# A gated delta recurrence: the state read through the keys, and its 16x16 inverses carried in another order

## The reference, cut to what matters

```python
    kb = kc * bc[..., None]
    lower = jnp.where(strict, jnp.einsum('nbhid,nbhjd->nbhij', kb, kc) * decay, 0.0)
    eye = jnp.broadcast_to(jnp.eye(CHUNK, dtype=F32), lower.shape)
    rhs = jnp.concatenate([vc * bc[..., None], kb * jnp.exp(gcum)[..., None]], axis=-1)
    sol = lax.linalg.triangular_solve(eye + lower, rhs, left_side=True, lower=True, unit_diagonal=True)
    u, w = sol[..., :dv], sol[..., dv:]
    ...
    def step(S, inp):
        q_i, k_i, u_i, w_i, a_i, g_i = inp
        v_new = u_i - jnp.einsum('bhck,bhkv->bhcv', w_i, S)
        o = (jnp.einsum('bhck,bhkv->bhcv', q_i * jnp.exp(g_i)[..., None], S)
             + jnp.einsum('bhij,bhjv->bhiv', a_i, v_new))
        g_last = g_i[..., -1]
        S = (S * jnp.exp(g_last)[..., None, None]
             + jnp.einsum('bhck,bhcv->bhkv', k_i * jnp.exp(g_last[..., None] - g_i)[..., None], v_new))
        return S, o
```

## Time and profile before

| what | before |
|---|---|
| median of 3 runs | 4209.69 us (4206.33 to 4217.25) |
| the profiled execution | 4213.43 us, its span 4211.7 us |
| PE busy | 3824.5 us (91%) |
| DVE, ACT, GpSimd busy | 43%, 23%, 8% |
| mean granted clock of PE | 0.951 |
| the two recurrences, from the start of pair 0 to the last product | about 210 us each |

### The profile page before, as it was taken

How to read it: one execution, slowest core, us unless ns; L and a number is a source line. 1 busy time by engine, 2 the same in 40 slices (tenths; PEclk the granted TensorE clock), 3 DMA queues, 4 the chain that set the end, 5 groups by cost and what they waited for, 6 DMA issues and landing times.

```text
span 4211.7 us, 50930 instructions
## 1 busy us (share of the span) xinstructions
PE 3824.5 (91%) x21420; PEld 2363.6 (56%) x21420; DVE 1826.8 (43%) x2843; ACT 966.6 (23%) x1894; POOL 356.2 (8%) x929
## 2 busy tenths in 40 slices
PE   8989899898899999899988989888888998998999
PEld 4578556874644434677776765222354433446777
DVE  3645445554211212478886540110236476415443
ACT  3421223222311111356554211000114200100000
POOL 0033001210100000000000000000040056100000
PEclk8989999999899999799998999999988999999999
DMA  5231122311398898122111436999921021231331
GB/s 196 86 113 55 50 100 73 111 59 51 130 379 338 342 380 320 72 81 80 52 34 37 130 120 248 421 421 421 362 62 61 21 55 50 75 100 50 110 100 51
DMA packets 278564, 631.32 MB, mean 150 GB/s; under 512 B 63552, under 2 KB 205376, under 8 KB 219456
## 3 DMA queue, kind: packets, MB, share of 16 engines
q1 hardware_dynamic: 275712, 627.40, 40.4%
q10 hardware_dynamic: 2624, 0.66, 0.1%
HBM read 611.75 MB, written 16.25 MB: 149 GB/s over the span
## 4 chain that ended last, share of the span: by engine, by line
PE 68%; DVE 11%; DMA 11%; ACT 3%; issue 3%; SPq 2%; POOL 2%; ACTq 0%; DVEq 0%
PE ps L1854 11%; PE ps L1559 11%; PE ps L1209 6%; PE ps L1905 5%; PE ps L1565 4%; DMA arena<-moe_w_down 4%; DMA arena<-moe_w_gate 2%; PE ps L1454 2%; PE ps L2078 2%; PE ps L1466 2%; PE ps L1712 2%; PE ps L1708 2%; PE ps L1717 2%; DMA arena<-moe_w_up 2%; DVE arena L3419 2%
## 5 line engine op out<-in xcount | busy, mean ns | idle before, releaser
L1559 PE MATMUL ps<-arena 128*64 128x512 f32 x3072 | 708.9, 602 | 79.2 <-DMA arena<-moe_w_up 22.4
L1559 PEld LDWEIGHTS ps<-arena 128*64 128x64 f32 x3072 | 207.9, 137 | 528.4 <-issue 385.3
L3157 DVE SCALAR_TENSOR_TENSOR arena<-arena,ps 128x512 f32<-128x512 f32 (+1 forms) x48 | 30.2, 656 | 525.7 <-PE ps L1559 525.7
L1209 PE MATMUL ps<-arena 128*128 128x512 f32 (+1 forms) x768 | 253.9, 489 | 3.5 <-DVE g_rows L2825 2.1
L1905 PE MATMUL ps<-arena 128*128 128x512 f32 x512 | 229.6, 606 | 5.0 <-DVE arena L3419 4.3
L3419 DVE TENSOR_TENSOR arena<-arena,ps 128x512 f32<-128x512 f32 x86 | 58.4, 687 | 370.8 <-ACT arena L2712 143.5
L1712 PE MATMUL ps<-h_first,w_rest 128*128 128x512 f32 (+1 forms) x576 | 214.4, 388 | 0.5 <-DVE arena L3318 0.5
L1209 PEld LDWEIGHTS ps<-arena 128*128 128x128 f32 x768 | 146.2, 191 | 105.4 <-issue 93.5
L3165 DVE TENSOR_TENSOR m_yx_rest<-ps,m_yx_lead 64x512 fp32r<-64x512 f32 x64 | 44.1, 688 | 362.0 <-ACT m_yc_lead L2426 205.4
L1708 PE MATMUL ps<-h_second,w_rest 128*128 128x512 f32 (+1 forms) x576 | 200.6, 364 | 0.4 <-DVE h_second L3223 0.4
L2426 ACT ACTIVATE m_yx_lead<-ps 64x512 fp32r<-64x512 f32 x64 | 37.8, 591 | 660.8 <-PE ps L1559 660.0
(11 more groups left out here) (499 smaller groups left out, 7073.7 us busy)
## 6 DMA issues: line engine op xcount, KB each, us to landing
arena<-moe_w_gate SPq DMA_DIRECT2D x128, 1024.0 KB, 9.0
arena<-moe_w_up SPq DMA_DIRECT2D x128, 1024.0 KB, 9.9
arena<-moe_w_down SPq DMA_DIRECT2D x128, 1024.0 KB, 11.2
arena<-ada_w SPq DMA_DIRECT2D x48, 1024.0 KB, 4.8
arena<-ffn_w_gate_up SPq DMA_DIRECT2D x22, 1024.0 KB, 5.0
arena<-gdn_w_in SPq DMA_DIRECT2D x16, 1024.0 KB, 9.6
arena<-w_in SPq DMA_DIRECT2D x30, 512.0 KB, 3.9
arena<-ssd_w_x SPq DMA_DIRECT2D x8, 1024.0 KB, 5.0
```

Source lines behind the costliest of these rows:

```text
L1209: mm = pe.matmul(ps[:, 2 * (i % 2) + j, 0:nn], state.w[:, k, m * P:(m + 1) * P], hT[:, k, c0:c0 + nn], start=(k == 0), stop=(k == KD - 1))
L1559: mm = pe.matmul(ps[CAPX * h:CAPX * h + CAPX, bank, :], x[:, 0:CAPX], w[:, 512 * h:512 * h + 512], **flags)
```

## The change

Two things. First, the order of the products: PE multiplies the keys with the state (`key_states`, into the bank in which T vB lay), DVE takes b e^g times that from `vB` (`less_state`, with the negative factors `nbeg`), and the inverse is applied once, to the difference (`values`). W, `kB` and ACT's negated copy go. `queries` moves ahead of `scaled_last` on DVE.

Second, the order of the DMAs. Each of the four steps becomes a function, and the counts of `r_low` come from a table `LOW_AT`, built from `low_order`. The matrix of the next pair is sent and awaited before the inverted blocks of this pair go out, and, from the second pair on, the blocks of the next pair are fetched before this pair's matrices come back. In the first pair of a recurrence the 8 inverted DMAs of the second unit are issued by ACT, behind its third `ada_row`. `EARLY` is issued when the matrices of the second pair are back.

```diff
+LOW_PARTS = {"matrix": 2, "blocks": 8, "inverted": 16, "back": 4}
+
+
+def low_order(first):
+
+    steps = [("matrix", first), ("blocks", first), ("matrix", first + 1), ("inverted", first), ("back", first), ("blocks", first + 1)]
+    for n in range(first + 1, first + PAIRS):
+        more = n + 1 < first + PAIRS
+        steps += [("matrix", n + 1)] * more + [("inverted", n)] + [("blocks", n + 1)] * more + [("back", n)]
+    return steps
...
-        LOW_DMAS, LOW_BASE = 16 * 30, 16 * 4
+        LOW_AT, landed = {}, 16 * 4
+        for hg in range(GH // HG):
+            for step in low_order(hg * PAIRS):
+                landed += 16 * LOW_PARTS[step[0]]
+                LOW_AT[step] = landed
...
-                for p in range(PAIRS):
-                    n = hg * PAIRS + p
-                    sp.wait_ge(s.r_low, LOW_DMAS * n + LOW_BASE)
+
+
+                first = hg * PAIRS
+
+                def matrix(n):
                     for u in range(2):
                         sp.wait_ge(s.r_xt, 2 * n + u + 1)
-                        sp.dma_start(A["low_in"][u], rX[2 * (p % 3) + u]).then_inc(s.r_low, 16)
-                    sp.wait_ge(s.r_low, LOW_DMAS * n + 32 + LOW_BASE)
+                        sp.dma_start(A["low_in"][u], rX[2 * ((n - first) % 3) + u]).then_inc(s.r_low, 16)
+                    sp.wait_ge(s.r_low, LOW_AT["matrix", n])
+
+                def blocks(n):
                     for u in range(2):
                         for j in range(HG):
                             src = blocks_of("low_in", u, j)
                             sp.dma_start((low[0], low[1])[u][32 * u + 8 * j:32 * u + 8 * j + 8, :].rearrange("b (r c) -> b r c", c=LOW), src).then_inc(s.r_low, 16)
-                    if p == 0:
-                        for item in GAP_LATE[hg]:
-                            load(item)
+
+                def inverted(n):
                     sp.wait_ge(s.r_el, n + 1)
-                    for u in range(2):
+                    for u in range(1 if n == first else 2):
                         for j in range(HG):
                             for x, name in enumerate(("low_u", "low_t")):
                                 sp.dma_start(blocks_of(name, u, j), low[2 + (x + u) % 2][32 * u + 8 * j:32 * u + 8 * j + 8, :].rearrange("b (r c) -> b r c", c=LOW)).then_inc(s.r_low, 16)
-                    sp.wait_ge(s.r_low, LOW_DMAS * n + 416 + LOW_BASE)
+
+                def back(n):
+                    p = n - first
                     if p == 0:
                         sp.wait_ge(s.gp_act, 24 * hg + 24)
                     if n >= 2:
@@ -906,7 +928,30 @@
                     for u in range(2):
                         sp.dma_start(rU[2 * (p % 2) + u], A["low_u"][u]).then_inc(s.r_low, 16)
                         sp.dma_start(rT[2 * (p % 2) + u], A["low_t"][u]).then_inc(s.r_low, 16)
-                    if p == 1:
+                    sp.wait_ge(s.r_low, LOW_AT["back", n])
+
+                matrix(first)
+                blocks(first)
+                for item in GAP_LATE[hg]:
+                    load(item)
+                sp.wait_ge(s.r_low, LOW_AT["blocks", first])
+                matrix(first + 1)
+                inverted(first)
+                sp.wait_ge(s.r_low, LOW_AT["inverted", first])
+                back(first)
+                blocks(first + 1)
+                for n in range(first + 1, first + PAIRS):
+                    if n + 1 < first + PAIRS:
+                        sp.wait_ge(s.r_low, LOW_AT["blocks", n])
+                        matrix(n + 1)
+                    inverted(n)
+                    if n + 1 < first + PAIRS:
+                        blocks(n + 1)
+                        sp.wait_ge(s.r_low, LOW_AT["blocks", n + 1])
+                    else:
+                        sp.wait_ge(s.r_low, LOW_AT["inverted", n])
+                    back(n)
+                    if n == first + 1:
...
-                    pool.wait_ge(s.r_low, LOW_DMAS * (n - 1) + 416 + LOW_BASE)
+                    pool.wait_ge(s.r_low, LOW_AT["inverted" if n % PAIRS < 2 else "blocks", n if n % PAIRS > 1 else n - 1])
                 g.settle()
                 g.do(pool.memset(w, 0.0))
                 g.settle()
                 g.do(pool.affine_select(out=w, in_=w, compare_op=ALU.not_equal, fill=1.0, base=0, pattern=[[1, LOW], [-1, LOW]], channel_multiplier=0))
-                pool.wait_ge(s.r_low, LOW_DMAS * n + 160 + LOW_BASE)
+                pool.wait_ge(s.r_low, LOW_AT["blocks", n])
...
-                def weights_w(p, u):
-
-                    n, b, z = hg * PAIRS + p, own(p, u), 2 * (p % 2) + u
-                    pe.wait_ge(s.r_kvs, 2 * n + u + 1)
+                def key_states(p, u):
+
+                    n, b = hg * PAIRS + p, own(p, u)
                     pe.wait_ge(s.r_u, 4 * n + 2 + u + 1)
-                    for j in range(HG):
-                        mm = pe.matmul(ps[:, b, heads[j]], kB[u][:, j, :], rU[z][:, j, :], start=True, stop=True)
-                    mm.then_inc(s.r_w, 1)
-
-                def values_own(p, u):
-
-                    n, b, z = hg * PAIRS + p, own(p, u), 2 * (p % 2) + u
-                    for j in range(HG):
-                        pe.matmul(ps[:, b + 1, heads[j]], rU[z][:, j, :], vB[u][:, j, :], start=(j == 0), stop=False)
-                    pe.wait_ge(s.r_tbq, n + 1)
-                    spread(tbq, u, side(p, u) + 1).then_inc(s.r_in2, 1)
-
-                def values_state(p, u):
-
-                    n, b = hg * PAIRS + p, own(p, u)
-                    pe.wait_ge(s.r_nw, 2 * n + u + 1)
                     if p:
                         pe.wait_ge(s.r_state, 2 * (n - 1) + u + 1)
+                    else:
+                        pe.wait_ge(s.r_kvs, 2 * n + u + 1)
                     for j in range(HG):
-                        mm = pe.matmul(ps[:, b + 1, heads[j]], rX[2 * (p % 3) + u][:, j, :], S[u][:, j, :], start=False, stop=(j == HG - 1))
+                        mm = pe.matmul(ps[:, b + 1, heads[j]], k_[:, j, chunk(p, u)], S[u][:, j, :], start=True, stop=True)
+                    mm.then_inc(s.r_w, 1)
+                    pe.wait_ge(s.r_tbq, n + 1)
+                    pe.wait_ge(s.r_kvs, 2 * n + u + 1)
+                    spread(tbq, u, side(p, u) + 1).then_inc(s.r_in2, 1)
+
+                def values(p, u):
+
+                    n, b, z = hg * PAIRS + p, own(p, u), 2 * (p % 2) + u
+                    pe.wait_ge(s.r_nw, 2 * n + u + 1)
+                    for j in range(HG):
+                        mm = pe.matmul(ps[:, b + 1, heads[j]], rU[z][:, j, :], vB[u][:, j, :], start=True, stop=True)
...
+                act.wait_ge(s.r_low, LOW_AT["matrix", hg * PAIRS + 1])
+                act.wait_ge(s.r_el, hg * PAIRS + 1)
+                for j in range(HG):
+                    for x, name in enumerate(("low_u", "low_t")):
+                        act.dma_start(blocks_of(name, 1, j), low[3 - x][32 + 8 * j:40 + 8 * j, :].rearrange("b (r c) -> b r c", c=LOW)).then_inc(s.r_low, 16)
                 for p in range(PAIRS):
                     n = hg * PAIRS + p
                     if p + 2 < PAIRS:
@@ -2332,9 +2376,6 @@
                         act.wait_ge(s.r_tu, 2 * (3 * n + 2) + u + 1)
                         a.do(act.activation(rU[2 * (p % 2) + u][one, :, two], ps[one, own(p, u) + 1, 0:64 * HG].rearrange("p (j c) -> p j c", j=HG),
                                             ACT.Copy, scale=-1.0), s.r_u)
-                    for u in units:
-                        act.wait_ge(s.r_w, 2 * n + u + 1)
-                        a.do(act.activation(flat(rX[2 * (p % 3) + u]), ps[:, own(p, u), :], ACT.Copy, scale=-1.0), s.r_nw)
...
-                    v.do(dve.tensor_tensor(kB[u], g3(side(p, u)), bc(beg[:, tile(p, u), i:i + HG]), ALU.mult))
                     v.do(dve.tensor_tensor(vB[u], g3(side(p, u) + 1), bc(beta[:, tile(p, u), i:i + HG]), ALU.mult), s.r_kvs)
+
+                def less_state(p, u):
+
+                    n, i = hg * PAIRS + p, 8 * u + hg * HG
+                    dve.wait_ge(s.r_w, 2 * n + u + 1)
+                    for j in range(HG):
+                        v.do(dve.scalar_tensor_tensor(out=vB[u][:, j, :], in0=ps[:, own(p, u) + 1, j * P:(j + 1) * P],
+                                                      scalar=nbeg[:, tile(p, u), i + j:i + j + 1], in1=vB[u][:, j, :], op0=ALU.mult, op1=ALU.add),
+                             s.r_nw if j == HG - 1 else None)
 
                 def scaled_last(p, u):
 
@@ -3025,10 +3074,13 @@
                             scores(p + 2, u)
                     for u in units:
                         scaled(p, u)
+                    v.settle()
+                    for u in units:
+                        less_state(p, u)
+                    for u in units:
+                        queries(p, u)
```

More of the change, by code:

```diff
@@ L453, in build @@
         beg = carve(NT, 16)
+        nbeg = carve(NT, 16)
         ea = carve(16)
@@ L458, in build @@
```

(21 more changed lines are left out.)

## The result

| | before | after |
|---|---|---|
| median of 6 runs each | 4214.20 us | 4238.48 us |
| ratio, 95% interval | | 1.0059 (1.0047 to 1.0071), slower by 0.6% |
| the profiled execution's span | 4211.7 us | 4241.5 us |
| PE busy | 3824.5 us | 3817.5 us |

The change takes work from PE and makes the program 24 us slower. The busy time by pair, from the start of a pair to the start of the next, answers to the earlier trace rows: length of the stretch, busy time of PE, PEld, DVE, ACT and GpSimd, granted clock, DMA share, GB/s.

A forecast was written before the change was run, and what follows sets the result against it. PE was taken to bound pairs 1, 3, 4 and 5, the DRAM round trip to bound ahead of pairs 0 and 2. Recurrences of +10.2 and +8.1 us, together +18.3 on the 4209.69 us median, gave 4228 us, range 4212 to 4248.

The forecast's parts named there:

- a loop through SyncE: SyncE awaits the next pair's matrix before this pair's inverted blocks, closing a 35.6 us loop at full clock; chance 0.62.
- pair 0 itself: Length of each recurrence's first pair, from its start to pair 1's: +2.5 us in the first, +2.4 in the second.
- The gaps: PE idles before each of pairs 1 to 4 of a recurrence, 5.0 us each; none before pair 5.
- The length of the loop: From one pair's start to the next where the loop binds: 18.4 + 2.6 + 17.2 = 38.2 us.
- the way after `r_xt`: From r_xt to the next pair's start: matrix, inverted blocks, next pair's blocks and DMAs back, taken as 17.2 us.
- The clock: PE runs at a lower clock after each 5 us gap, losing 2.6 us, with 1.4 and 2.9 as ends.
- PE's share: The new products save PE 2.5 us a pair, bounds 1.8 and 2.7.
- two starts: Within PE's saving per pair: two starts that no longer drain before a wait, 0.4 us.
- Pair 0's start: Each recurrence's first pair starts 6.2 us later, as ACT's 8 inverted DMAs wait behind its third ada_row.
- the transfers are hidden: Rival: PE alone sets the pace in both recurrences; -42 us, 4168 us; chance 0.10.
- The low end: Rival: the loop binds with every piece at its smallest size; 4212 us, all up to 4222; chance 0.20.
- the long low clock: Rival: each of 8 gaps costs 5.9 us of clock instead of 2.6; +26 us, 4254 us; chance 0.08.

The follow-up runs named there:

- e1_products: The kernel before with only the new products (key_states, less_state, values), DMAs in the old order: 1.0009 of before.
- e3_one_queue: The whole change, but SyncE issues all 16 inverted DMAs of pair 0: 1.0037 of the kernel before.
- e4b_together: Kernel before with new products, next matrix sent right behind the way back, no ACT half, EARLY loads two at a time: 4164.90 us, 0.9888.
- e2_queue: The kernel before with only the new order of the DMAs, ACT's half included, and the old products: 1.0065 of before.

## Why the prediction was right

I forecast +18.3 us, by a loop through SyncE; measured were 24 us, by that loop. The traces split the two sums like this: later starts of pair 0, +12.4 forecast and +13.0 measured; pair 0 itself, +4.9 and +11.8; pairs 1 to 5, +1.0 and -0.9. So the difference is nearly all in pair 0. The steps, with what the traces show for each (recurrences one and two):

- **The gaps.** "Some 5 us before each of pairs 1 to 4": 6.4, 6.4, 5.3, 4.9 and 6.5, 5.9, 5.7, 4.9 us. Pair 5 without one: right.
- **The length of the loop.** 38.2 us from start to start: 40.0, 37.8, 37.2 and 39.3, 38.3, 37.1 us for pairs 1 to 3. Their mean, 38.3, is closer than its parts, which is luck: from a pair's start to `r_xt` they take 20.4 us in the mean instead of 21.0, and the way after `r_xt`, taken as 17.2, takes 17.8 (18.7, 17.6 and 17.2 us before pairs 2 to 4 of the first recurrence). The way back alone takes 5.6 us instead of 5.2 before most pairs. Before pair 2 the blocks take 3.93 us to issue instead of 2.9, as one of the eight issues lasts 1.35 us instead of 0.33. `EARLY` is not shown to be the reason: such a pause also stands before pair 1, when no load of it has been issued, and in the kernel before.
- **The clock.** Taken as 2.6 us a gap; the rows of pairs 1 to 4 of the first recurrence lose 4.8, 1.9, 1.5 and 1.7 us (length times one minus the clock), 2.5 in the mean, though part of it falls into the gap itself. Until `r_xt`, which is what the loop pays, pairs 1 to 3 lose 2.1 us in the mean (20.4 - 18.4).
- **PE's share.** 2.5 us a pair: pair 5 takes 27.11 instead of 29.60 us, and a pair without gaps 30.56 instead of 33.11 (`e1_products`). That confirms the sum; of its terms no run shows the 0.4 us for two starts by itself. `less_state` takes 344 ns for 128x128, where 0.34 was extrapolated, and 27.1 / 96 = 0.28 us one behind another, where 0.26 was:

```profile
L2995 DVE SCALAR_TENSOR_TENSOR arena<-ps,arena 128x128 f32<-128x128 f32 x96 | 27.1, 344 | 6.9 <-PE ps L1398 6.9
```

- **Pair 0's start.** +6.2 each: from the last operand of pair 1's matrix to PE's start it takes 18.4 and 18.3 us instead of 11.8 and 11.9, +6.7 and +6.4. Here the way back took 5.7 and 5.6 us instead of 5.2. Without ACT's half it takes 14.7 and 16.2 us (`e3_one_queue`), so 3.8 and 2.1 us of it are that half.
- **What was mis-sized.** Pair 0 itself: +2.5 and +2.4 were forecast, +4.0 and +7.8 came. In the second recurrence I had carried over the 21.0 us to `r_xt` from before, a start after a gap of 4.2 us; now it takes 24.7 us, after a gap of 10.5 us. The first recurrence's 24.9, after a gap of 4.0 us, had shown that this was possible, and I had no ground to expect the lower value. The rest is the way after `r_xt`, 18.75 and 18.8 us instead of 17.2: the 16 issues took 7.0 and 6.9 us instead of 5.8, with pauses in them whose cause I did not find, and the way back 5.6 instead of 5.2.

The rival that the transfers are hidden is refuted by the waits; `e4b_together` shows what hidden transfers give once the order allows it, -47 us. My -42 is no match for that: it holds 12.4 us of later starts through ACT's half, which this kernel leaves out, and without them it is -55. The low end (+2 to +12 us) did not come, nor the long low clock after each gap; the latter came about once in each recurrence, in pair 0. The runs of one kernel scatter by 10 us and more, and what follows the recurrences took between 3277 and 3288 us in the traces, so single differences of under 5 us in the totals carry nothing.

## What to carry to other kernels

On a queue that works in order, a transfer sent ahead of time may only stand before an urgent one if its own operand is ready first; ask for every wait which engine produces what it waits for, and in which round. Work taken from an engine counts for nothing until the gap behind it is closed: here the products alone gave nothing measurable, the loads moved alone 30 us, both together 37 us, and both with an order that holds nothing urgent back 47 us. When a gap closes, the next longest way shows, so work out the length of every loop, not only of the one that binds.

## What the runs showed of the hardware

The clock after a gap does not follow from the length of the gap alone. After gaps of 9.8 to 11.0 us pair 0 needed between 21.0 us (`e2_queue`, granted clock 0.96 over the pair) and 24.9 us (the changed kernel, 0.81) to `r_xt`; in the kernel before it needed 24.9 us after a gap of 4.0 us. (The Trainium skill, TensorE: Matmul & The Clock Gate, "What's actually happening", says that the gate's watch runs freely and does not start with the kernel; the scatter agrees with that, and no run here isolates it.) The mean loss of 2.5 us was a usable price all the same.

A small DMA's issue on SyncE takes 0.33 us in the median, but single ones take over 1 us, in the kernel before as well. Its inverted blocks (count, then shortest, median and longest issue in ns):

```profile
L900 SPq DMA_DIRECT2D low_u<-arena x96: 264/327/1556, 224.2 to 893.9; - x96
```

What causes these pauses stays open. On a path that nothing hides, such as this loop, each one is paid in full.
